# Five matmuls for each weight block instead of six: token parts of 284 and 236, one part's low sums kept apart and added later

## The reference, cut to what matters

```python
def conv_ffn(h, conv_prev, w_up, conv_w, conv_b, w_down):
    t = h.shape[1]
    a = h @ w_up
    ap = jnp.concatenate([conv_prev.astype(a.dtype), a], axis=1)
    c = conv_b + ap[:, 0:t] * conv_w[0]
    for k in range(1, CONV_W):
        c = c + ap[:, k:k + t] * conv_w[k]
    g, u = jnp.split(c, 2, axis=-1)
    return (jax.nn.gelu(g, approximate=True) * u) @ w_down, ap[:, t:]
```

## Time and profile before

| | |
|---|---|
| time, median of 3 runs | 1464.67 us (1464.09 to 1467.34) |
| profiled execution: span from the first to the last instruction | 1461.2 us |
| TensorE busy | 1409.3 us (96%) |
| VectorE busy | 894.1 us (61%) |
| ScalarE busy | 536.8 us (37%) |
| TensorE's share of the chain that ended last | 91% |

### The profile page before, as it was taken

How to read it: one execution, slowest core, us unless ns; L and a number is a source line. 1 busy time by engine, 2 the same in 40 slices (tenths; PEclk the granted TensorE clock), 3 DMA queues, 4 the chain that set the end, 5 groups by cost and what they waited for, 6 DMA issues and landing times.

```text
span 1461.2 us, 30495 instructions
## 1 busy us (share of the span) xinstructions
PE 1409.3 (96%) x11815; PEld 1329.9 (91%) x11815; DVE 894.1 (61%) x1518; ACT 536.8 (37%) x870; POOL 175.0 (12%) x329
## 2 busy tenths in 40 slices
PE   6999999998999999999999989998999999999997
PEld 5999999998999999999989855657999999999997
DVE  4444664227888888633375686464578888884334
ACT  4545443236222223333464212344543222223334
POOL 1000000000222222100001020100012322321000
PEclk9999999999999999999999999799999999999999
DMA  7332222321332232233425463101223233222331
GB/s 232 103 86 73 73 75 82 91 87 48 97 100 87 86 100 80 78 96 89 119 69 187 176 248 125 48 1 34 83 60 100 86 94 92 86 77 88 92 90 65
DMA packets 224370, 138.20 MB, mean 95 GB/s; under 512 B 12620, under 2 KB 220674, under 8 KB 223256
## 3 DMA queue, kind: packets, MB, share of 16 engines
q1 hardware_dynamic: 219688, 112.38, 26.5%
q0 software_dynamic: 4224, 24.62, 4.5%
q10 hardware_dynamic: 384, 0.16, 0.1%
HBM read 133.83 MB, written 3.67 MB: 94 GB/s over the span
## 4 chain that ended last, share of the span: by engine, by line
PE 91%; DVE 5%; ACT 2%; issue 1%; DMA 1%; SPq 0%; DVEq 0%; ACTq 0%
PE psum L659 76%; PE psum L1054 2%; PE psum L1183 1%; PE psum L1160 1%; PE psum L1037 1%; PE psum L718 1%; PE psum L1015 1%; PE psum L818 1%; PE psum L1163 1%; DVE ut L1686 1%; DVE x L1689 1%; DVE kt L1978 1%; DMA xn<-in_x_prompt 1%; PE psum L1172 1%; DVE wl L1647 1%
## 5 line engine op out<-in xcount | busy, mean ns | idle before, releaser
L1647 DVE TENSOR_TENSOR wl<-ws,wh 128x1024 fp32r<-128x1024 f32 x217 | 265.8, 1225 | 336.5 <-ACT wh L1243 173.5
L659 PE MATMUL psum<-xh,wh 128*128 128x260 f32 x2064 | 426.6, 285 | 11.0 <-DVE xl L1666 6.2
L659 PE MATMUL psum<-xh,wl 128*128 128x260 f32 x2064 | 421.5, 283 | 0.0
L659 PE MATMUL psum<-xl,wh 128*128 128x260 f32 x2064 | 420.6, 283 | 0.0
L659 PEld LDWEIGHTS psum<-xh,wh 128*128 128x128 f32 x2064 | 320.9, 189 | 14.3 <-issue 13.5
L659 PEld LDWEIGHTS psum<-xh,wl 128*128 128x128 f32 x2064 | 320.6, 189 | 0.0
L659 PEld LDWEIGHTS psum<-xl,wh 128*128 128x128 f32 x2064 | 320.0, 188 | 0.4
L1243 ACT ACTIVATE wh<-ws 128x1024 fp32r<-128x1024 f32 x144 | 152.2, 1057 | 319.1 <-PE psum L659 319.1
L659 PE MATMUL psum<-acth,wh 128*128 128x260 f32 x704 | 144.3, 284 | 0.0
L659 PE MATMUL psum<-acth,wl 128*128 128x260 f32 x704 | 143.2, 282 | 0.0
L659 PE MATMUL psum<-actl,wh 128*128 128x260 f32 x704 | 143.0, 282 | 0.0
(11 more groups left out here) (283 smaller groups left out, 1812.9 us busy)
## 6 DMA issues: line engine op xcount, KB each, us to landing
ws<-in_w_up SPq DMA_DIRECT2D x88, 512.0 KB, 3.8
ws<-in_w_in_a SPq DMA_DIRECT2D x32, 512.0 KB, 4.1
ws<-in_w_down SPq DMA_DIRECT2D x32, 384.0 KB, 3.4
ws<-in_w_down SPq DMA_DIRECT2D x32, 320.0 KB, 3.1
ws<-in_w_out_a SPq DMA_DIRECT2D x16, 512.0 KB, 3.9
ws<-in_w_o SPq DMA_DIRECT2D x8, 512.0 KB, 4.6
xn<-in_x_prompt SPq DMA_DIRECT2D x4, 512.0 KB, 10.1
ws<-in_w_dq SPq DMA_DIRECT2D x4, 512.0 KB, 4.6
```

The lines of the kernel that those rows point to most:

```text
L659: mm = pe.matmul(psum[:, 2 * slot + b, 0:HB], w, r[:, k, b * HB:(b + 1) * HB], start=st, stop=en)
L1647: dve.tensor_tensor(low_, ws[:, slot4, :], f32(high), ALU.subtract).then_inc(w_low, 1)
```

## The change

It does four things.

1. The token halves become parts of WA = 284 and WB = 236 tokens, everywhere. The first part's sums stand at the end of the accumulator's first bank and the second part's at the start of the second, so that `acc` is one stretch of 520 columns.
2. High and low data become one tensor (`xhl`, `ushl`, `acthl`, ...), so that one moving operand can take the second part of both. In units with `apart`, a block's high weights meet that part's high and low data in one matmul of 2 x 236 = 472 columns; the low data's sums gather in 236 columns of their own in the second bank. A block so takes 5 matmuls, of 472, 284, 284, 284 and 236 columns: again 1560 in all. Units that run part by part, the third latent tile and the `U_UQ` units keep 6 matmuls, now of 284 and 236 columns.
3. When such a unit (or the last unit of a tile) is done, ScalarE copies the low sums to `lows` (`copy_low`), and VectorE adds them to the second part's sums in PSUM (`fold`), before those are read.
4. The three steps of the convolution stay on VectorE; the first one signals a semaphore of its own (`conv_first`). `cc` shares memory with `sq`, and some small tensors move.

The core of the diff:

```diff
-HB = T // 2
+WA, WB = 284, 236
...
+        def part(slot, h):
+
+            return psum[:, 2 * slot + 1, 0:WB] if h else psum[:, 2 * slot, 512 - WA:512]
+
+        def part_and_low(slot):
+
+            return psum[:, 2 * slot + 1, 0:2 * WB]
+
+        def low_part(slot):
+
+            return psum[:, 2 * slot + 1, WB:2 * WB]
...
-            def product(n, slot, nslot, k, kk, rh, rl, first, last, parts=(0, 1)):
+            def product(n, slot, nslot, k, kk, rhl, first, last, parts=(0, 1), apart=False):
+
+                rh, rl = rhl[:, 0, k, :], rhl[:, 1, k, :]
...
+                if apart:
+                    pe.matmul(part_and_low(slot), hw, rhl[:, :, k, HALF[1]], start=first, stop=False, skip_group_check=True)
                 for w, r, st, en in ((hw, rh, first, False), (hw, rl, False, False), (lw, rh, False, last)):
                     for b in parts:
-                        mm = pe.matmul(psum[:, 2 * slot + b, 0:HB], w, r[:, k, b * HB:(b + 1) * HB], start=st, stop=en)
+                        if not (apart and b and w is hw):
+                            mm = pe.matmul(part(slot, b), w, r[:, HALF[b]], start=st, stop=en, skip_group_check=apart and b == 1)
                 return mm
...
+            def copy_low(done, slot, b):
+
+                act.wait_ge(mm_done, done)
+                act.activation(lows[:, b, :], low_part(slot), ACT.Copy).then_inc(low_copied, 1)
+
...
+            def fold(stage, t, slot, b):
+
+                dve.wait_ge(low_copied, FOLD[stage] + t + 1)
+                dve.tensor_tensor(part(slot, 1), part(slot, 1), lows[:, b, :], ALU.add).then_inc(folded, 1)
...
-                    a_b = psum[:, 4:6, :] if second else psum[:, 2 * b:2 * b + 2, :]
-                    dve.tensor_tensor(ab[:, b, 2:2 + HB], a_b[:, 0, 0:HB], r1[:, 0:HB], ALU.mult)
-                    dve.tensor_tensor(ab[:, b, 2 + HB:2 + SEQ], a_b[:, 1, 0:SEQ - HB], r1[:, HB:SEQ], ALU.mult)
...
+                    slot = 2 if second else b
+                    dve.tensor_tensor(ab[:, b, 2:2 + WA], part(slot, 0), r1[:, 0:WA], ALU.mult)
+                    if not isinstance(q, int) or q >= 2:
+                        fold(f"up{l}", q - 2, slot, b)
+                        dve.wait_ge(folded, FOLD[f"up{l}"] + q - 1)
+                    dve.tensor_tensor(ab[:, b, 2 + WA:2 + SEQ], part(slot, 1)[:, 0:SEQ - WA], r1[:, WA:SEQ], ALU.mult)
...
-                    dve.tensor_scalar(cc[:, b, :], ab[:, b, 0:CW_], w[0], bias, ALU.mult, ALU.add).then_inc(conv_step, 1)
-                    dve.wait_ge(conv_step, 2 * Q + 1)
+                    dve.tensor_scalar(cc[:, b, :], ab[:, b, 0:CW_], w[0], bias, ALU.mult, ALU.add).then_inc(conv_first, 1)
+                    dve.wait_ge(conv_first, Q + 1)
```

More of the change, by code:

```diff
@@ L671, in unit, with first_units @@
                         between[kk]()
-                    mm = product(n, slot, nslot, k, koff + kk, rh, rl, first and kk == 0, last and kk == len(ks) - 1)
+                    mm = product(n, slot, nslot, k, koff + kk, rhl, first and kk == 0, last and kk == len(ks) - 1, apart=apart)
                 mm.then_inc(mm_done, 1)
-            def first_units(n, rh, rl, sem, before_half, between):
+            def first_units(n, rhl, sem, before_half, between):
                 pe.wait_ge(w_low, n + 2)
@@ L871, in wo_tile @@
                 for half in range(1 if last else 2):
-                    unit(U_WO + 2 * t + half, weight_slot(U_WO + half), e, range(half * KD, (half + 1) * KD), ush, usl, half == 0, half == 1,
-                         ready=[(usl_ready, 0)] if first else None)
+                    unit(U_WO + 2 * t + half, weight_slot(U_WO + half), e, range(half * KD, (half + 1) * KD), ushl, half == 0, half == 1,
+                         ready=[(usl_ready, 0)] if first else None, apart=not last)
                     if first and half == 0:
@@ L915, in down @@
                     for w, (k0, kc) in enumerate(DN_SPLIT[:3] if last else DN_SPLIT):
-                        unit(U_DN[l] + 4 * t + w, weight_slot(U_DN[l] + w), e, range(k0, k0 + kc), acth, actl, w == 0, w == 3,
-                             ready=[(actl_ready, KF * l)] if first else None)
+                        unit(U_DN[l] + 4 * t + w, weight_slot(U_DN[l] + w), e, range(k0, k0 + kc), acthl, w == 0, w == 3,
+                             ready=[(actl_ready, KF * l)] if first else None, apart=not last)
                     if last:
@@ L956, in _ @@
             for b in range(2):
-                mm = pe.matmul(psum[:, 4 + b, 0:HB], perm, krr[:, b * HB:(b + 1) * HB], start=True, stop=True)
+                mm = pe.matmul(part(2, b), perm, krr[:, HALF[b]], start=True, stop=True)
             mm.then_inc(rotk_done, 1)
@@ L1464, in down @@
                     t = 2 * i + e
+                    last = isinstance(t, int) and t == KD - 1
                     for w in range(4):
+                        if w == 3 and not last:
+                            copy_low(U_DN[l] + 4 * t + 4, e, e)
                         if guard:
@@ L1813, in wo @@
                     for half in range(2):
+                        if half and not (isinstance(t, int) and t == KD - 1):
+                            fold("wo", t, e, e)
                         ahead(U_WO, 4, i, 2 * e + half)
@@ L1893, in down @@
                     for w in range(4):
+                        if w == 3 and not (isinstance(t, int) and t == KD - 1):
+                            fold(f"dn{l}", t, e, e)
                         if guard:
```

223 lines of the change are left out of this document (131 added, 92 removed).

## The result

The changed kernel takes 1476.42 us (median of 4 runs, 1476.23 to 1478.14), beside 1466.01 for the kernel before in the same runs: a ratio of 1.0079, 95% interval 1.0065 to 1.0093. It is slower by 0.8%. 1470 was forecast, within 1447 to 1487. The profiled span went from 1461.2 to 1474.4, +13.2, where the sum of the prediction had +5.2.

What follows compares the result with a forecast made beforehand. TensorE, busy 96% of the span, bounds the kernel, with VectorE becoming the bound in the up-projection. +8.4 - 6.0 + 0.7 + 2.1 = +5.2 takes the span from 1461.2 to 1466.4; median 1470 us, range 1447 to 1487.

Steps and rivals of the forecast that it cites:

- TensorE's block: Five-matmul blocks were to take 8 ns less each; 748 of them outside the up-projections give -6.0 us.
- (a): Reading of TensorE's fp32r matmul pitch: a fixed 11.6 ns beside N/2.4; a five-matmul block changes by -10.5 ns.
- (b): Reading of TensorE's fp32r matmul pitch: a slower stream, 0.461 ns a column; a five-matmul block changes by +2.1 ns.
- Blocks that keep six matmuls: 188 blocks with six matmuls of uneven parts were to cost +3.2 ns each, +0.7 us in all.
- Up-projection: VectorE becomes the bound at 11.65 us a pair of tiles; +4.2 us a layer, +8.4 for two.
- Elsewhere the copy and fold lie beside units: Outside up-projections and seams, copy (0.36 us) and fold (0.43) were taken as hidden beside units of 3.6 to 7 us.
- Seams: Three stage ends at 0.5 us each for a longer first part, plus 0.6 at the last query tile: +2.1 us.
- 1 (weights set the pace): The weight load sets the matmul pace on TensorE, some -38 ns a block; about 1447 us, chance 0.15.
- 4 (two runs): Reading the moving operand as two runs slows the long matmul, +3.5 ns a block outside up-projections; 1479 us, chance 0.05.
- 2 (VectorE keeps up): In the up-projection half of VectorE's added 0.70 us is hidden, below 11.38 a pair; 1456 us, chance 0.12.
- 3 (a longer pair): Up-projection pair 0.4 us above 11.65; sign: fold waits over 0.6 for `lows` in odd tiles; 1486 us, chance 0.20.
- 5 (four passes for few columns): Fp32r with few columns falls back to four passes, 393 ns for 111 in 1608 blocks; about 1900 us, chance 0.03.

Runs made afterwards that it cites:

- e5: Changed kernel plus a list of back-to-back fp32r matmuls on data at rest, before the last transposes; 260 columns take 119 ns, 472 in two runs 214.
- e1: Changed kernel with six matmuls a block everywhere, parts still 284 and 236, no copies or additions; ratio 1.0103 to the kernel before, span 1472.6 us.
- e6: Changed kernel with the convolution's first step moved from VectorE to ScalarE; ratio 1.0037 to the kernel before, span 1469.5 us.
- e2: Changed kernel with its five matmuls but no copy or addition, leaving out those low sums; ratio 1.0009 to the kernel before, span 1461.3 us.
- e7: Changed kernel with the low sums' copy behind the rounding of weights on ScalarE, gate side only; ratio 1.0081 to the kernel before, span 1472.5 us.
- e8: Changed kernel with parts of 264 and 256 tokens; median 1473.72 us, ratio 1.0065 to the kernel before.
- e9: Changed kernel with parts 264 and 256, convolution's first step on ScalarE, gate side with six matmuls and no copy or addition; 1458.33 us, ratio 0.9953.
- e10: Changed kernel with parts 264 and 256, convolution's first step on ScalarE, gate side's copy behind the rounding of weights; 1459.87 us, ratio 0.9965.

## Why the prediction was right or wrong

- **TensorE's block, forecast -8 ns, measured about -1, and -4 in the down-projections.** This is the step that failed first: I took a value near reading (a). The record lengths of fp32 matmuls, which spoke for (a), are of another type, and e5 shows that fp32r has a pace of its own: 0.452 ns a column. By (b) I had +2.1, and the trace of after has medians of 217, 3 x 131 and 109 to 110: 720. Between the ends it lay, but near (b), not near (a). What the blocks gave shows as 0.7 us (in the gate's output and the down-projections), where 748 blocks were to give 6.0.
- **Blocks that keep six matmuls, +3.2 ns each:** measured +12 in e1, so an estimate of 188 x 12 ns = 2.3 us and not 0.7. The floor was placed about right (111; e5 has 112 for 236 columns), its effect in a row of uneven matmuls was not known. These blocks lie in the first and last units of stages, which is part of the value side's and the seams' losses.
- **Up-projection, +4.2 a layer, measured +3.3 and +3.4.** The mechanism and its parts were right, VectorE's list as the new bound included (e6): the even tile grew from 4.85 to 5.30 us (388.57 - 383.27; forecast +0.43), the odd one's `wl` comes 0.25 later (forecast +0.27), pair 11.60 for 11.65, tile 4 to tile 8 23.22 for 23.3. The copy takes 361 ns and the addition 407, for 0.36 and 0.40. Each 0.05 of the pair is 1 us a layer.
- **"Elsewhere the copy and fold lie beside units, on engines with over half of their time free."** This is the second step that failed, in the gate side: nothing was put down for it, and it cost 3.7 us over 13 units, or an estimated 4.2 to 4.6 for all 16 at 0.26 to 0.29 each. The sentence rested on the down-projection's row; in the gate side VectorE was busy for 59.09 of 91.70 us (64%), and above all the chain's slack was 0.40 and 0.77 was put into it. The rows for that slack were in the trace of before. e2 (7.08 us a unit for 7.34) shows the price, e7 (7.22) that a part of it hangs on the copy's place in ScalarE's list.
- **Seams, +2.1.** The sum is near (+1.8, +2.2 and -1.4), the cause is not. Most of it is TensorE's clock, as below.
- **The rivals.** 1 (weights set the pace) and 4 (two runs) are out by e5; 2 (VectorE keeps up) by the changed kernel's trace, where no reading waits for TensorE, and by e6; 3 (a longer pair) by 11.60, although its sign of 0.6 was there; 5 (four passes for few columns) by 109 to 112 for 236.

The missed terms add up to the difference: 5.2 + 5.3 (gain that did not come) + 3.7 (gate side) + 1.6 (blocks of six) - 1.7 (up-projections) = 14.1, beside 13.2 measured. The seams (+0.5), attention (+0.8), its output (-0.5) and the rest of the value side are not in this sum, so it closes to 1 or 2 us only. All of these but the last had one sign. That 1476.42 still lies within 1463 to 1478, the range of my own case, is luck: its upper end came from a block that loses 2.1 ns everywhere, which none did, and was reached by the gate side and the blocks of six instead.

## What to carry to other kernels

A step is hidden only if the chain that it joins has slack: follow one tile from the end of its matmuls to the next instruction that TensorE waits for, and compare with the unit's length, before a busy share is read as room. Fewer matmuls win little where a column's pace is the bound (0 to 4 ns of 720 a block here). An uneven split that takes some matmuls under the floor (here some 240 columns of fp32r) costs more than that: 12 ns a block of six matmuls in the up-projection. Parts that stay above it and fill the long matmul to its 512 won 10 ns a block in the up-projection and 3 in the down-projection, and the kernel must then find the time for what it adds on the engine that comes next. Where two readings of a pitch differ in the sign of the result, no row of another data type should decide between them.

## What the runs showed of the hardware

**Short stretches at half clock decide the seams.** The first 12 matmuls of the latent stage, behind the same wait for `xkhl` (2.63 us in the changed kernel, 2.40 in e8). Windows from their first start to the norm's first matmul, of the changed kernel and of e8:

```profile
742.34:745.32 2.98, 2.98 (x13) 2.98 (x13) 2.88 (x6) 2.19 (x5) 0.00 (x0) 0.50 0.00 0
```

```profile
737.61:739.13 1.52, 1.52 (x12) 1.52 (x13) 1.42 (x3) 1.25 (x3) 0.00 (x0) 1.00 0.00 0
```

The granted clock is 0.50 in the one, 1.2 GHz, and 1.00 in the other, 2.4 GHz, and the same 12 matmuls take 1.5 us longer (of which e8's 20 columns fewer explain 0.1). Such stretches, of 11 to 22 matmuls, lie at one to four places of a kernel outside attention and the very end, and not at the same ones: near 140 in e1 to e5, e9 and e10, but not in the kernel before or the changed one; at 342 in the changed kernel and in e2 but not in e7; at 371 in e6, which is what layer 0 did not get back; at 1051 in the kernel before and not in the changed one, which is its -1.4 in that seam. I did not try to move one on purpose.

**Attention takes 111.8 to 119.7 us with the same instructions.** Timeline, TensorE, from the first `uk` matmul to the first `pp` one, of e1 and of e8:

```profile
834.80 1.91 PE L1037 MATMUL psum<-cst,uk 128*128 128x128 f32 x16
...
945.34 0.44 PE L1209 MATMUL psum<-cst,pp 128*128 128x128 f32 x2
```

```profile
826.93 1.91 PE L1037 MATMUL psum<-cst,uk 128*128 128x128 f32 x16
...
944.71 0.44 PE L1209 MATMUL psum<-cst,pp 128*128 128x128 f32 x2
```

110.5 and 117.8 us. Over the whole stage, 111.8 us in e1 and 119.6 in e7, the granted clock was 0.93 and 0.89, but it was also 0.93 in e6 with 114.9 and 0.89 in the kernel before with 116.4: it follows the time only roughly, and what sets the time stays open. The spread is as large as what was being measured: e1's total would be 4.6 us worse with the attention of before, and e10's 3.4 better. For kernels that differ by less than 0.3% here, stage by stage is the comparison that can be trusted, the total is not.

**Open:** why a column of fp32r takes 0.452 ns at 2.4 GHz, where it takes what the lower clock asks at 1.2 GHz; and why a block of 512, 264, 264, 264 and 256 columns takes 711 ns at rest and 710 in the up-projection, where 0.452 ns a column and 2 fixed give 715, and 718 in the down-projection.
